# A two-stage fp32 transformer block on one core: order of the first norm, places of the modulation slabs, casts inside the gate chain, order of two up-projections

## The reference

```python
for layer in range(2):                                  # first block
    h = rms_norm(x, norm_w[layer])
    q, k, v, z, q_h, f_h, i_h, g_h, gate_attn, gate_hgrn = split(h @ w_in[layer])
    a = sliding_window_attention(rope(q), rope(k), v, sinks[layer]) * silu(z)
    logf = log(lb + (1 - lb) * sigmoid(f_h));  kin = (1 - lb) * sigmoid(-f_h)
    b = norm(hgrn2_recurrence(silu(q_h), kin, i_h, logf)) * silu(g_h)
    merged = sigmoid(gate_attn) * (a @ w_up_attn[layer]) + sigmoid(gate_hgrn) * (b @ w_up_hgrn[layer])
    x = x + merged @ w_out[layer]
x = rms_norm(x, final_norm_w)
mod = silu(c) @ ada_w + ada_b                           # 2 layers x 6 sections of 1024
for i in range(2):                                      # second block
    h = x * (1 + sc_t) + sh_t
    y = dsa_mixer(h) if i == 0 else diff_mixer(h)       # top-64 sparse / differential attention
    x = layer_norm(ALPHA * x + (1 + g_t) * y)
    h = x * (1 + sc_c) + sh_c
    x = layer_norm(ALPHA * x + (1 + g_c) * square(relu(h @ w1)) @ w2)
```

## Time and profile before

| | |
|---|---|
| median of 3 runs | 1339.19 us (1336.64 to 1339.91) |
| profiled execution | 1346.1 us, span 1344.0 us |
| mean granted TensorE clock | 0.893 of full |
| busy: PE, PEld | 1131.1 us (84%), 954.6 us (71%) |
| busy: DVE, ACT, POOL | 483.0 (36%), 550.8 (41%), 743.7 us (55%) |
| HBM read | 219.48 MB, 164 GB/s over the span |
| chain that ended last | PE 67%, DVE 14%, ACT 7%, DMA 4%, issue 3%, POOL 3% |

### The profile page before, as it was taken

One profiled execution on the slowest core, in us unless ns is written; L12 is line 12 of the kernel. 1 busy time (PEld: TensorE's weight loads), 2 busy tenths in 40 slices (PEclk: granted clock), 3 DMA queues, 4 the chain that ended last, 5 costly groups with the idle time before them and its releaser, 6 DMA issues.

```text
span 1344.0 us, 15901 instructions
## 1 busy us (share of the span) xinstructions
PE 1131.1 (84%) x6584; PEld 954.6 (71%) x6584; DVE 483.0 (36%) x689; ACT 550.8 (41%) x749; POOL 743.7 (55%) x341
## 2 busy tenths in 40 slices
PE   2789698787796988879889699999698657999995
PEld 0778576656685766669678698888687446899894
DVE  3426633232457152323752511113600564301114
ACT  2455354323544363344442344344224432444441
POOL 1475362744464554646204487778457206588883
PEclk9899899897897988989857899999799668899997
DMA  7365333745461535475302366775287203456550
GB/s 282 119 248 190 128 124 114 243 176 178 177 238 65 188 105 208 147 245 157 126 0 66 99 230 231 278 261 180 92 302 272 88 0 126 153 181 195 175 174 32
DMA packets 101022, 221.58 MB, mean 165 GB/s; under 512 B 11360, under 2 KB 17878, under 8 KB 94806
## 3 DMA queue, kind: packets, MB, share of 16 engines
q1 hardware_dynamic: 95776, 210.29, 45.9%
q10 hardware_dynamic: 5174, 10.28, 2.1%
HBM read 219.48 MB, written 1.07 MB: 164 GB/s over the span
## 4 chain that ended last, share of the span: by engine, by line
PE 67%; DVE 14%; ACT 7%; DMA 4%; issue 3%; POOL 3%; ACTq 1%; POOLq 0%; DVEq 0%; SPq 0%
PE lin_ps L321 12%; PE lin_ps L322 11%; PE lin_ps L323 11%; PE tmp_ps L328 5%; PE tmp_ps L330 5%; PE tmp_ps L329 5%; PE tmp_ps L376 3%; PE lin_ps L328 3%; POOL wlo L805 3%; PE tmp_ps L419 2%; PE lin_ps L329 2%; PE lin_ps L330 2%; PE tmp_ps L516 2%; DMA ring<-in_b_w_in 2%; ACT whi L880 2%
## 5 line engine op out<-in xcount | busy, mean ns | idle before, releaser
L805 POOL TENSOR_TENSOR wlo<-ring,whi 128x1024 fp32r<-128x1024 f32 (+2 forms) x304 | 724.6, 2396 | 484.3 <-ACT whi L880 483.3
L880 ACT CAST whi<-ring 128x1024 fp32r<-128x1024 f32 (+2 forms) x304 | 312.6, 1035 | 534.2 <-PE lin_ps L323 244.2
L321 PE MATMUL lin_ps<-whi,hThi 128*128 128x512 f32 (+2 forms) x528 | 212.3, 402 | 27.2 <-POOL wlo L805 12.1
L322 PE MATMUL lin_ps<-wlo,hThi 128*128 128x512 f32 (+2 forms) x528 | 206.3, 391 | 0.0
L323 PE MATMUL lin_ps<-whi,hTlo 128*128 128x512 f32 (+2 forms) x528 | 205.9, 390 | 0.0
L328 PE MATMUL tmp_ps<-hThi,whi 128*128 128x256 f32 x520 | 149.5, 287 | 4.9 <-DVE hTlo L1517 4.9
L330 PE MATMUL tmp_ps<-hThi,wlo 128*128 128x256 f32 x520 | 148.7, 286 | 0.0
L329 PE MATMUL tmp_ps<-hTlo,whi 128*128 128x256 f32 x520 | 148.7, 286 | 0.0
L321 PEld LDWEIGHTS lin_ps<-whi,hThi 128*128 128x128 f32 x528 | 103.4, 196 | 60.1 <-issue 20.8
L328 PE MATMUL lin_ps<-hThi,whi 128*128 128x256 f32 x352 | 106.8, 303 | 30.2 <-POOL wlo L805 18.1
L323 PEld LDWEIGHTS lin_ps<-whi,hTlo 128*128 128x128 f32 x528 | 102.8, 195 | 20.8
(11 more groups left out here) (246 smaller groups left out, 1514.2 us busy)
## 6 DMA issues: line engine op xcount, KB each, us to landing
ring<-in_mlp_w SPq DMA_DIRECT2D x64, 1024.0 KB, 5.3
ring<-in_ada_w SPq DMA_DIRECT2D x48, 1024.0 KB, 5.5
ring<-in_w_in SPq DMA_DIRECT2D x40, 1024.0 KB, 5.3
ring<-in_b_w_in SPq DMA_DIRECT2D x12, 1024.0 KB, 5.7
ring<-in_w_out SPq DMA_DIRECT2D x8, 1024.0 KB, 5.2
ring<-in_a_w_in SPq DMA_DIRECT2D x6, 1024.0 KB, 5.8
ring<-in_w_up_hgrn SPq DMA_DIRECT2D x4, 1024.0 KB, 6.1
ring<-in_w_up_attn SPq DMA_DIRECT2D x4, 1024.0 KB, 9.8
```

Of the source, the lines that this page charges most:

```text
L321: pe.matmul(ps, xh, hi, start=first, stop=False, skip_group_check=True)
L322: pe.matmul(ps, xh, lo, start=False, stop=False, skip_group_check=True)
L805: pool.tensor_tensor(wlo[:, n % PARTS, :, 0:width], ring[:, u % RING, 2 * h:2 * h + 2, 0:width], whi[:, n % PARTS, :, 0:width].bitcast(F32 ...
L880: act.copy(whi[:, n % PARTS, :, 0:width], ring[:, u % RING, 2 * h:2 * h + 2, 0:width]).then_inc(S("high_formed"), 1)
```

## The change

- The first layer starts without slabs: TensorE's `ada(4)` stands only in layer 1. On ScalarE the square of x and the first three casts come first; csil, the gate-bias loads and the sine go behind Silu of qh, the two small exps stand ahead of the gate chain, the store of relvec behind q. On VectorE the small parameters are taken behind the scaling of x, and the angle, lb and lambda steps stand behind x's low parts. The relvec matmul goes behind kv. SyncE loads one unit and then waits for x before the others. GpSimd waits for the scaling before it goes on to subtractions (both layers).
- `ahead` takes a number of further halves; two more calls stand inside the gate chain.
- The visit of four behind the attention is gone in both layers, and `uh0`, `uh1` go ahead of the transposes aT.
- A visit of four stands at the boundaries s0, s1 and s2, ahead of TensorE's wait for x; a group is closed behind the index projection of s0.

The slabs per place, f0 to s2: before 16, 16, 0, 8, 8 (layer 0, layer 1, s0, s1, s2), after 8, 12, 4, 12, 12.

```diff
+ADA_BOUNDARIES = ("s0", "s1", "s2")
             # TensorE
-            pe.wait_ge(S("small_landed"), 16 * 10)
+            pe.wait_ge(S("small_landed"), 16 * 9)
...
-            ps = open_tmp("relvec")
-            pe.wait_ge(S("rel_landed"), 32)
-            close_tmp(pe.matmul(ps[0:16, 0, 0:DIST], relT[:], onehot[:], start=True, stop=True), "relvec")
...
-                if L == 0:
-                    pe.wait_ge(S("csil"), 1)
-                ada(4)
+                if L:
+                    ada(4)
                 pe.wait_ge(S("f_scaled"), L + 1)
                 feature_major(f"f{L}hT", hs)
...
                 linear_tok(f"f{L}kv", w, K0, 256, hT)
+                if L == 0:
+                    ps = open_tmp("relvec")
+                    pe.wait_ge(S("rel_landed"), 32)
+                    close_tmp(pe.matmul(ps[0:16, 0, 0:DIST], relT[:], onehot[:], start=True, stop=True), "relvec")
+                    pe.wait_ge(S("csil"), 1)
                 ada(2)
...
-                ada(4)
-                pe.wait_ge(S("f_a"), L + 1)
-                feature_major(f"f{L}aT", hs[:, :, 0:HALF], 4)
-
                 wait_read(f"f{L}bT0")
                 for c in range(2):
                     linear_tok(f"f{L}uh{c}", I["w_up_hgrn"][L], c * HALF, HALF, hT, kts=4, k_src=4)
+                pe.wait_ge(S("f_a"), L + 1)
+                feature_major(f"f{L}aT", hs[:, :, 0:HALF], 4)
                 wait_read(f"f{L}aT0")
...
             def mixed(name):
 
+                if name in ADA_BOUNDARIES:
+                    ada(4)
                 pe.wait_ge(S(f"{name}x"), 1)
...
             linear_feat("s0iq", w, 1280, hT)
 
+            ada_close()
             wait_read("s0ik", "s0iq")
             # SyncE
             for n, unit in enumerate(units):
+                if n == 1:
+
+                    sp.wait_ge(S("x_landed"), 16)
             # GpSimd
             rstd("f0", row, one)
+            pool.wait_ge(S("f_scaled"), 1)
             rstd("f0h", st[:, 1], st[:, 2], "f0ho")
             rstd("f1", row, one, "f0out1")
+            pool.wait_ge(S("f_scaled"), 2)
             # ScalarE
-                          allow_slow_non_contiguous=True).then_inc(S("small_landed"), 16)
+                          allow_slow_non_contiguous=True).then_inc(S("posi_landed"), 16)
...
-            def ahead(name):
+            def ahead(name, more=0):
 
-                high_parts(halves_at[name][0] + PARTS, halves_at[name][1])
+                high_parts(halves_at[name][0] + PARTS + more, halves_at[name][1])
...
                 if L == 0:
-                    for j in range(2):
-                        gate_bias(0, j)
                     squares("f0", (S("x_landed"), 16))
+                    high_parts(PARTS, 0)
+                    act.wait_ge(*read_of("cols"))
...
+                if L == 0:
+                    act.wait_ge(S("lb_max"), 1)
+                    act.activation(lbw[:, 0:2, :], lbw[:, 0:2, :], ACT.Exp).then_inc(S("lb_exp"), 1)
+                    act.wait_ge(S("lam_dots"), 1)
+                    act.activation(lams[:, 0:2], lams[:, 0:2], ACT.Exp).then_inc(S("lam_exp"), 1)
                 ahead(f"f{L}f")
                 act.wait_ge(*read_of(f"f{L}f"))
                 act.activation(gate_p[:], gate_min[:], ACT.Exp)
                 act.activation(gate_n[:], gate_max[:], ACT.Exp, scale=-1.0).then_inc(S("f_pn"), 1)
+                ahead(f"f{L}f", 1)
                 act.wait_ge(S("f_sum"), L + 1)
...
                 ins.then_inc(S("f_ln"), 1)
+                ahead(f"f{L}f", 2)
                 act.wait_ge(S("f_kexp"), L + 1)
...
                 read(act.activation(flat(qin), flat(ps), ACT.Silu), f"f{L}qh")
+                if L == 0:
+                    act.activation(csil[:], colA[:, 120:128].unsqueeze(2).broadcast_to([P, KT, ADA_ROWS]), ACT.Silu
+                                   ).then_inc(S("csil"), 1)
+                    for j in range(2):
+                        gate_bias(0, j)
+                    act.wait_ge(S("angles"), 1)
+                    act.activation(trig[:], ang[:], ACT.Sin).then_inc(S("trig"), 1)
...
+                if L == 0:
+                    act.wait_ge(*read_of("relvec"))
+                    act.dma_start(scratch, relvec).then_inc(S("scratch_written"), 16)
             # VectorE (the angle, lb and lambda steps move as they are)
                 ins.then_inc(S("f_scaled"), 1)
-                ada()
+                if L:
+                    ada()
+                else:
+                    ps = full_tmp_of(dve, "cols")
+                    dve.tensor_copy(colA[:], ps[:, 0, 0:P])
+                    read(dve.tensor_copy(colB[:], ps[:, 0, P:P + 5 + 8 * KT]), "cols")
...
                 dve.tensor_tensor(hs[:, :, 0:HALF], hs[:, :, 0:HALF], zs[:], ALU.mult).then_inc(S("f_a"), 1)
-                ada()
-                low_of(f"f{L}aT0", 0)
...
                     read(dve.tensor_tensor(gh[:, :, cols], ps, gh[:, :, cols], ALU.mult), f"f{L}uh{c}")
+                    if c == 0:
+                        low_of(f"f{L}aT0", 0)
...
             ins.then_inc(S("s0x"), 1)
+            ada()
...
                 ins.then_inc(S(f"{after}x"), 1)
+                if after in ADA_BOUNDARIES:
+                    ada()
...
             ins.then_inc(S("s0ckvn"), 1)
+            ada_close()
```

More of the change, by code:

```diff
@@ L1200, in _ @@
-            for part in TURN_PARTS:
-                step(dve.scalar_tensor_tensor(ang[:], angk[:], -part, ang[:], ALU.mult, ALU.add))
-            step(dve.tensor_scalar(ang[:, :, 1, :], ang[:, :, 1, :], TURN / 4, None, ALU.add))
-            dve.tensor_scalar(ang[:], ang[:], SIN_MAX, -SIN_MAX, ALU.min, ALU.max).then_inc(S("angles"), 1)
-            step(dve.tensor_copy(lbw[:, 0:2, :], colA[:, 16:24].rearrange("p (l h) -> p l h", l=2)))
-            step(dve.tensor_tensor(lbw[:, 2, :], lbw[:, 0, :], lbw[:, 1, :], ALU.max))
@@ L1307, in _ @@
                            [colA[:, 8 * L + k:8 * L + k + 1] for k in range(4 * h, 4 * h + 4)])
+                if L == 0:
+                    dve.wait_ge(S("posi_landed"), 16)
+                    dve.wait_ge(S("invf"), 1)
+                    step(dve.tensor_copy(posf[:], posi[:]))
+                    for i in range(NT):
+                        for c in range(2):
+                            ins = dve.tensor_scalar(ang[:, i, c, :], invf[:], posf[:, i:i + 1], None, ALU.mult)
+                    step(ins)
+                    for c in range(2):
+                        ins = dve.tensor_scalar(angk[:, :, c, :], ang[:, :, c, :], 1.0 / TURN, 0.25 * c, ALU.mult, ALU.add)
+                    step(ins)
+                    step(dve.tensor_scalar(angk[:], angk[:], ROUNDER, None, ALU.add))
+                    step(dve.tensor_scalar(angk[:], angk[:], -ROUNDER, None, ALU.add))
+                    for part in TURN_PARTS:
+                        step(dve.scalar_tensor_tensor(ang[:], angk[:], -part, ang[:], ALU.mult, ALU.add))
+                    step(dve.tensor_scalar(ang[:, :, 1, :], ang[:, :, 1, :], TURN / 4, None, ALU.add))
+                    dve.tensor_scalar(ang[:], ang[:], SIN_MAX, -SIN_MAX, ALU.min, ALU.max).then_inc(S("angles"), 1)
+                    step(dve.tensor_copy(lbw[:, 0:2, :], colA[:, 16:24].rearrange("p (l h) -> p l h", l=2)))
+                    step(dve.tensor_tensor(lbw[:, 2, :], lbw[:, 0, :], lbw[:, 1, :], ALU.max))
+                    dve.tensor_tensor(lbw[:, 0:2, :], lbw[:, 0:2, :], lbw[:, 2, :].unsqueeze(1).broadcast_to([P, 2, 4]),
+                                      ALU.subtract).then_inc(S("lb_max"), 1)
+                    dve.wait_ge(S("lb_exp"), 1)
+                    step(dve.tensor_tensor(lbw[:, 2, :], lbw[:, 0, :], lbw[:, 1, :], ALU.add))
+                    step(dve.reciprocal(lbw[:, 2, :], lbw[:, 2, :]))
+                    step(dve.tensor_tensor(lbw[:, 0:2, :], lbw[:, 0:2, :], lbw[:, 2, :].unsqueeze(1).broadcast_to([P, 2, 4]),
+                                           ALU.mult))
+                    step(dve.tensor_tensor(lbw[:, 3, :], lbw[:, 0, :], lbw[:, 1, :], ALU.add))
+                    step(dve.tensor_tensor(lbw[:, 3, :], lbw[:, 3, :], lbw[:, 0, :], ALU.subtract))
+                    step(dve.tensor_scalar(lbw[:, 4, :], lbw[:, 3, :], -1.0, 1.0, ALU.mult, ALU.add))
+                    dve.wait_ge(S("lamb_landed"), 16)
+                    for n in range(2):
+                        step(dve.tensor_tensor(lamb[:, 2 * n, :], lamb[:, 2 * n, :], lamb[:, 2 * n + 1, :], ALU.mult))
+                        ins = dve.tensor_reduce(lams[:, n:n + 1], lamb[:, 2 * n, :], AX.X, ALU.add)
+                    ins.then_inc(S("lam_dots"), 1)
+                    dve.wait_ge(S("lam_exp"), 1)
+                    step(dve.tensor_tensor(lams[:, 2:3], lams[:, 1:2], lams[:, 0:1], ALU.subtract))
+                    step(dve.tensor_scalar(lams[:, 3:4], lams[:, 2:3], -LAM_INIT, None, ALU.add))
+                    step(dve.tensor_scalar(lams[:, 4:5], colB[:, 2:3], 1.0 - LAM_INIT, None, ALU.mult))
@@ L1337, in _ @@
```

(3 more changed lines are left out.)

47 lines of the change are left out of this document (removed).

## The result

| | before | after |
|---|---|---|
| median | 1339.55 us, 4 runs (1336.64 to 1342.23) | 1305.11 us, 4 runs (1302.41 to 1306.76) |
| profiled execution, span | 1346.1, 1344.0 us | 1302.41, 1300.7 us |
| granted clock | 0.893 | 0.913 |

The ratio is 0.9741 (95% interval 0.9715 to 0.9768): 34.4 us less where 50 were forecast. A second measurement of the same kernel gave 0.9743 (0.9706 to 0.9779).

The account below looks back on a forecast made before the run. TensorE's gaps, from late normalised x at boundaries and late low halves, were taken as the bound. 22 + 2.8 + 6.4 + 5 + 13 + 6.5 - 6 = 49.7 us off a 1339.2 us median gave 1289 us, range 1270 to 1310.

Parts of the forecast that it names:

- Start, 22 net: Kernel start: x's norm first brings the first product at 18.0 instead of 43.51 us; 25.5 less a stall, net 22.
- I take 4.2 at the granted full level: Start: first transpose to first product takes 4.2 us at full clock, against 5.4 us before at the lower clock.
- 2 MB take 5.6 us: Start: with one ring load beside x, 2 MB move in 5.6 us, so x lands at about 7.5 to 8.
- Gate chain, 2.8 and 6.4: Gate chain: casting high halves inside it removes the wait at qh's last half; 2.8 us layer 0, 6.4 layer 1.
- Level 6, 5: Level 6, layer 0: no slab group closes there, so the visit no longer waits for its buffer; gain 5 us.
- Rival C: Level chain swallows the gains of the gate chain and level 6; 14 us come back, 1303 us; chance 0.08.
- Up-projection, 6.4 per layer: Behind the attention: up-projection ahead of the transposes, with weights and three halves ready; 6.4 us per layer, 13 in all.
- Boundaries: Slabs at block boundaries: f1 gains 6.5 us; s0, s1 and s2 together lose 6 us.
- +4 for Mbias: Boundary s0: the 2 MB of Mbias share the wires, adding 4 us.
- Rival B: Boundaries s0, s1, s2 each go as f1's did, 20.1 us; 16 us more, 1305 us; chance 0.12.
- Rival A: Start gives half, since several things must come together: gain 11 instead of 22 us, 1300 us; chance 0.13.
- E: Whole kernel: more than 60 us gained, as shrinking gaps also keep the clock up; 1277 us; chance 0.05.

Follow-up runs that it names:

- e9: Changed kernel without SyncE's wait for x, so all four first weight loads are issued at once beside x; 1301.93 us, ratio 0.9695.
- e4: Changed kernel without the two extra cast calls inside the gate chain; 1307.90 us, ratio 0.9759.
- e8: Changed kernel with ScalarE's two gate-bias loads of layer 0 put behind q instead of behind Silu of qh; 1302.57 us, ratio 0.9711.
- e3: Changed kernel with the casts inside the gate chain moved one step forward; 1298.33 us, ratio 0.9696.
- e5: Changed kernel with the transposes aT put back ahead of the recurrent branch's up-projection, the visit of four staying away; 1300.87 us, ratio 0.9697.
- e12: The combined kernel e11 with the transposes aT ahead of the up-projection again; 1280.72 us, ratio 0.9546.
- e1: Changed kernel with the 2 MB position-bias load moved from boundary s0 to behind the second pair of index scores; 1298.70 us, ratio 0.9678.
- e2: Changed kernel with ScalarE taking hT after one cast instead of three at every boundary; 1295.43 us, ratio 0.9669.
- e11: Changed kernel with the edits of e1, e2, e3 and e8 joined, plus earlier casts of f0's fourth and fifth halves; 1280.42 us, ratio 0.9555.
- e10: The changed kernel itself, unedited, measured again; 1306.59 us, ratio 0.9743.
- e6: Changed kernel with the visit of four of boundary s0 put back behind the attention of layer 1; 1303.15 us, ratio 0.9710.
- e7: Changed kernel without GpSimd's two waits for the scaling of x (f0, f1); 1307.30 us, ratio 0.9742.

## Why the prediction was right, and where it was not

The time lay in the range (1270 to 1310), 16 us above the point, and 5 us outside the forecast's own range (1277 to 1300), so it was the width given to the rivals that held it. Against the profiles the sum was 49.7 and 43.3 came, of which 7 lie in s0's attention, where the forecast had nothing; so the terms brought about 14 us less than their sum. The large gains, at the start and at f1, are read from the two profiles; no run undoes them alone.

1. **Start, 22 net.** Right in kind: 22.5 - 0.5 measured in place of 25.5 - 4. x was scaled at 13.8, as worked out; the table load ahead of the square took 1.28 us (7.88 to 9.17). Of the 1.5 us to start the trace shows this: x was issued at 0.80, the DMA share stayed at 0 until 1.6 and read 1.00 from 3.2 to 4.0. The first product was 3 us later: "I take 4.2 at the granted full level" failed. It rested on the 1.00 of the earlier trace rows, under which the slabs at 20.53 already ran at near half pace (6.44 us against 3.64), and the transposes did so again (3.49 us against 1.94). And ScalarE's third cast (16.68 to 17.73) stood ahead of hT because its load waited for x; e9 gets 1.5 us back. The small loads were in at 10.22, not 13. The stall at the fourth half was 0.48, not 4; the small exps came at 25.6 and 27.95. The step "2 MB take 5.6 us" gave the right landing by luck, for a reason that e9 refutes.
2. **Gate chain, 2.8 and 6.4.** The failed term: 2.4 us in all, not clear of nothing (e4). The qh waits went, as forecast, and from f's end to kv's end layer 0 took 20.9 us (21.3 forecast). But I priced new waits inside kv only, at the end of the chain, and stopped there. In layer 1 kv's halves wait twice (2.50, 2.30), and q's weights come late behind them (2.00), since kv frees their slot. In layer 0 q's weights took 2.8 us longer to land than in e8, which made a wait of 2.79 us and q's start at the lower level (0.57 granted from 61 to 64 us). The gate-bias loads, "taken as nothing", have a part in it, but e9 has them and not the delay, so the cause is open. e3 shows that the cast's place in the queue mattered: one step earlier brings 3 and 4.7 us against the change's profile (about 2 in each layer against the shortest such stage of a kernel without this edit).
3. **Level 6, 5.** Measured 6.3 us, with the mechanism as told. Rival C (the chain swallows the rest) is refuted: the wait at level 6 is 6.8 to 7.0 us in every kernel here.
4. **Up-projection, 6.4 per layer.** The part brought 5.7 and 3.4 us between the attention's end and the last product of w_out (65.7 to 60.0 and 66.1 to 62.7; in the executions where this stage took 60.0, layer 1 gains 6 as well), less 2.9 ahead of the attention's end. The 10.0 us were rightly read, but what removed them is that the visit and its weights' wait are gone; the order is worth nothing (e5, e12). Not foreseen: with no visit in the way, ScalarE now casts inside the attention (198.40 to 199.46 in layer 0), so its copy of the last probabilities comes late and the last product with v waits 0.97 us. That explains a part of the 2.9.
5. **Boundaries.** f1: last to first product 21.55 to 13.5, a gain of 8.05 for 6.5. s1 and s2: 16.1 and 16.2 us, for a forecast of 16 and 16, with the residual's last step alone (1.23 us at s1, 3.34 before) and s1's first hTlo beside GpSimd (3.25 us, 1.23 without), as told. s0: 20.4, not 17. The step "+4 for Mbias" was right in size: the 2 MB added 4.3 us to the weights' landing, and e1 gets 4.4 back. What the sum had at nothing is the way behind that landing: it added the 4 to the time of x (13.0), though the earlier trace rows had shown that three casts stand between late weights and hT. At s0 they do: taking hT behind one of them brings 3.7 us (e2), both edits together 8.2 (e11).

Rival B names the measured time, 1305, but not its mechanism: only s0 went nearly as B has it (20.4 us for 21.6). Rival A is refuted by the first product at 21.0. D, a kernel slower than before by a lower granted clock, is refuted by the ratio and by that clock, which rose from 0.893 to 0.913. The clock rose as E has it, but not the gain to 60 us.

## What to carry to other kernels

When casts are moved forward in an in-order queue, follow the freed and the taken slots through to the next load: the wait doesn't end with the first result that is on time, it moves to whatever is formed or loaded next (here from 13.2 us ahead of qh's last halves to 11.5 at kv and q). At a boundary, let the evacuation on the critical path stand ahead of preparations for later halves (3.7 us at s0, e2), and keep large loads that nobody needs yet away from the moment when a drained ring refills (4.4 us at s0, e1). And compare stage by stage before crediting a difference between two profiles to the edit: one stretch differed by 4.6 us between two executions of the same kernel. When one edit takes a wait away, look for a second one that does so with the suspect in place, as e9 did to e8.

## What the runs showed of the hardware

- The mean granted clock in s0's attention took few values over all 14 profiles of nearly the same work: 0.50 (the kernel before), 0.58 (e3, e4, e9, e10), 0.63 (e2, e6, e7, e8, e11) and 0.74 to 0.79 (the change, e1, e5, e12), with 42.4, 40.3, 38.0 and 35.4 to 35.8 us. Ahead of this stage TensorE had small matmuls with gaps of up to 4.3 us (4.24 in the kernel before, 3.83 in the change). What decides when the clock rises again was not found.
- The clock column said 1.00 from the span's start to about 20 us of the changed kernel, while 16 transposes took 3.49 us there; in the kernel before they took 3.67 under 0.50, and in the change 1.94 at f1 under 1.00.
- x of 1 MB landed after 7.2 us beside four loads of projection weights (e9) and after 10.4 beside four slabs (the kernel before), all of 1 MB.
- 2 MB on one queue put the landing of the first 1 MB on another from 6.7 to 11.0 us after its issue (e1 and the change).
